# Two heads or two softmaxes at a time in the attentions of a two-block transformer kernel

## The reference

```python
def softmax_attend(q, k, v, scale):
    s = einsum('bqhd,bkhd->bhqk', q, k) * scale
    return einsum('bhqk,bkhd->bqhd', softmax(s), v)

# window heads: |qpos - kpos| <= 128 among latent keys, all 256 context keys, one sink column
p = softmax(concatenate([s_ctx, where(valid, s_band, NEG_INF), sink_col], -1))

def diff_attend(q, k, v, lam, lambda_init, subln_g):
    s = einsum('bqhtd,bkhtd->bthqk', q, k) * HEAD_DIM ** -0.5
    p = softmax(s)
    a = p[:, 0] - lam * p[:, 1]
    o = einsum('bhqk,bkhe->bqhe', a, v)
    return rms_norm(o, subln_g) * (1.0 - lambda_init)
```

## Time and profile before

| | us |
|---|---|
| median of 3 runs | 4892.38 (4888.57 to 4893.21) |
| the profiled execution, device time | 4884.59 |
| its span, first to last instruction | 4882.8 |
| full heads of layer 0, stretch 2941 to 3112 | 171.0 |
| window heads of layer 0, stretch 3112 to 3279.5 | 167.5 |
| differential attention, stretch 4229 to 4363 | 134.0 |

### The profile page before, as it was taken

The page is one execution under the profiler, slowest core; times in us unless marked ns, Lnnn a source line. Parts: engine busy times, 40 slices in busy tenths (PEclk is TensorE's granted clock), DMA queues, the critical chain, the costliest instruction groups (busy, mean ns, idle before and its releaser), DMA issues.

```text
span 4882.8 us, 51549 instructions
## 1 busy us (share of the span) xinstructions
PE 4490.2 (92%) x20694; PEld 3482.8 (71%) x20694; DVE 2612.7 (54%) x4643; ACT 1512.5 (31%) x2535; POOL 1738.0 (36%) x955
## 2 busy tenths in 40 slices
PE   7878989987789999999999899997999979998998
PEld 3667745465668888888888675665888857765886
DVE  4675745368867676754534415654334350484334
ACT  3212211035753232232322324443222232343222
POOL 2244332036954444444444321002222225103442
PEclk9998999998899999999999999988999989998999
DMA  6200200421265554545533200001222112102331
GB/s 219 70 26 14 109 31 31 146 74 62 121 224 173 177 171 162 178 157 174 173 125 129 87 14 21 9 14 39 65 63 68 57 34 61 34 1 62 98 95 48
DMA packets 170762, 441.31 MB, mean 90 GB/s; under 512 B 12219, under 2 KB 78971, under 8 KB 167580
## 3 DMA queue, kind: packets, MB, share of 16 engines
q1 hardware_dynamic: 168060, 422.61, 25.7%
q0 software_dynamic: 2464, 15.41, 0.8%
HBM read 402.32 MB, written 35.65 MB: 90 GB/s over the span
## 4 chain that ended last, share of the span: by engine, by line
PE 68%; DVE 10%; POOL 3%; ACT 2%; issue 1%; DMA 0%; DVEq 0%; ACTq 0%; POOLq 0%
PE psum L254 19%; PE psum L255 19%; PE psum L256 19%; PE psum L260 11%; POOL o L1600 2%; DVE st L2209 2%; PE psum L281 1%; DVE o L1493 1%; DVE Pd L2235 1%; DVE X L1882 0%; ACT P L2280 0%; DVE o L1495 0%; DVE Pe L2233 0%; DVE ffl L1822 0%; DVE rstd L1862 0%
## 5 line engine op out<-in xcount | busy, mean ns | idle before, releaser
L244 POOL TENSOR_TENSOR pair<-raw_ring,pair 128x1024 fp32r<-128x1024 f32 x502 | 1243.2, 2490 | 2063.2 <-ACT pair L236 2063.1
L236 ACT CAST pair<-raw_ring 128x1024 fp32r<-128x1024 f32 x502 | 509.9, 1045 | 374.4 <-PE psum L256 318.6
L254 PE MATMUL psum<-pfh,pair 128*128 128x512 f32 x1152 | 451.7, 392 | 27.3 <-POOL pair L244 26.5
L1675 DVE SCALAR_TENSOR_TENSOR h<-psum,mods,h 128x512 f32<-128x512 f32 x512 | 370.8, 748 | 162.6 <-PE psum L256 160.8
L255 PE MATMUL psum<-pfl,pair 128*128 128x512 f32 x1152 | 449.9, 391 | 0.0
L256 PE MATMUL psum<-pfh,pair 128*128 128x512 f32 x1152 | 449.9, 391 | 0.0
L254 PE MATMUL psum<-ffh,pair 128*128 128x512 f32 (+1 forms) x1056 | 378.3, 358 | 45.7 <-DVE ffl L1822 45.7
L254 PE MATMUL psum<-Ah,pair 128*128 128x512 f32 x1024 | 400.9, 391 | 10.1 <-DVE Al L1670 4.9
L255 PE MATMUL psum<-Al,pair 128*128 128x512 f32 x1024 | 400.4, 391 | 0.0
L256 PE MATMUL psum<-Ah,pair 128*128 128x512 f32 x1024 | 400.2, 391 | 0.0
L255 PE MATMUL psum<-ffl,pair 128*128 128x512 f32 (+1 forms) x1056 | 378.7, 359 | 0.0
(11 more groups left out here) (552 smaller groups left out, 9136.1 us busy)
## 6 DMA issues: line engine op xcount, KB each, us to landing
raw_ring<-wmod SPq DMA_DIRECT2D x144, 512.0 KB, 4.9
raw_ring<-peeru SPq DMA_DIRECT2D x128, 512.0 KB, 4.2
raw_ring<-peerv SPq DMA_DIRECT2D x128, 512.0 KB, 3.9
gates<-stage SPq DMA_DIRECT2D x16, 2048.0 KB, 6.4
Gb<-gates SPq DMA_DIRECT2D x32, 1024.0 KB, 9.2
raw_ring<-win SPq DMA_DIRECT2D x48, 512.0 KB, 4.4
raw_ring<-wgate SPq DMA_DIRECT2D x44, 512.0 KB, 3.5
raw_ring<-wup SPq DMA_DIRECT2D x44, 512.0 KB, 3.6
```

The costliest lines, as they stand in the source:

```text
L236: ac.e.copy(self.pair(t)[0], k.R.of(t)).then_inc(*k.A.up("hi", t))
L244: po.e.tensor_tensor(lo, k.R.of(t), hi.bitcast(F), ALU.subtract).then_inc(*k.G.up("lo", t))
L254: e.matmul(out, w[0], x[0], start=first, stop=False, skip_group_check=True)
L1675: e.scalar_tensor_tensor(out=h[:, j, :], in0=B.of(("down", gi, j)), scalar=m[:, 40 + j, 0:1], in1=h[:, j, :], op0=ALU.mult, op1=ALU.add).t ...
```

## The change

Units of layer 0 become 48 pairs: of the full heads two heads, of the window heads the two key groups kv = 0 and 1 (w = 0 and 1 in the code). Their values go to the two column halves of one output tile, product by product in turn. Where queries and keys are 64 rows deep (window heads and layer 1, `apart`), the score products of w = 0 and w = 1 alternate, so that they use rows 0 to 63 and 64 to 127 in turn. Band masks are added by a product with the identity, and the sink becomes one more score column, also by a product. Scale factors are applied when queries are copied out. The maximum is negated by the reduction itself. ScalarE copies whole transposed rows in layer 0. Output is copied per unit (128 columns) and not per head. Query and key buffers grow to four heads, exponentials to six buffers, transposed rows to three; the first three heads are prepared before the first scores.

In layer 1 nothing is divided by the first softmax's sum: the row becomes e1 + (-lambda x sum1 / sum2) x e2, and the sum enters the epsilon of the norm that follows (three small steps, one each on TensorE, ScalarE and VectorE). For odd units VectorE makes this with one operation, for even units GpSimd makes it with two. Transposes are split in four and two pieces, with the values of unit i-3 between, and all of them share banks 6 and 7, so that the six other banks serve scores alone.

The core of the diff (removed lines are those of the functions printed above and are left out; so are the new buffers):

```diff
+        self.keys = sum(p[3] for p in pieces[0])
+        self.n = self.keys + (sinks is not None)
...
+        return self.st[(2 * i + w) % len(self.st)]
+    def pt(self, i, w):
+        return self.PT[(2 * i + w) % len(self.PT)]
...
+    many = 1 if u.n <= 512 else 2
+    banks = [B.take((key, "s", i, w), many, SIX) for w in range(2)]
+    def masked(w):
+        for c, mk in u.masks:
+            ins = mm(e, banks[w][:, c:c + 128], k.sq["ident"], k.sq[mk], False, True)
+        if u.sinks is not None:
+            ins = mm(e, banks[w][:, u.keys:u.n], k.sq["ident"], u.sinks[w])
+        return ins
+    if u.apart:
+        pe.wait_ge(B.free((key, "s", i, 0)), B.free((key, "s", i, 1)))
+        for j in range(len(u.pieces[0])):
+            for w in range(2):
+                q, kk, c, n = u.pieces[w][j]
+                ins = mm(e, banks[w][:, c:c + n], q, kk)
+                if u.sinks is None and j == len(u.pieces[0]) - 1:
+                    ins.then_inc(*P.up(key, "s", i, w))
+        if u.sinks is not None:
+            for w in range(2):
+                masked(w).then_inc(*P.up(key, "s", i, w))
+    else:
+        for w in range(2):
+            pe.wait_ge(B.free((key, "s", i, w)))
+            for q, kk, c, n in u.pieces[w]:
+                ins = mm(e, banks[w][:, c:c + n], q, kk)
+            ins.then_inc(*P.up(key, "s", i, w))
...
+    dv.e.tensor_reduce(s[:, 0:1], k.B.of((at.key, "s", i, w))[:, 0:at.units[i].n], AX, ALU.max, negate=True).then_inc(*k.V.up(at.key, "m", i, w))
...
+    ac.e.activation(p[:, 0:u.n], k.B.of((at.key, "s", i, w))[:, 0:u.n], AF.Exp, bias=s[:, 0:1], accum_out=total).then_inc(*k.A.up(at.key, "e", i, w))
+    k.B.over((at.key, "s", i, w), k.A.now())
...
+        bank = B.take((key, "pt", i, w), 1 if u.keys <= 512 else 2, SIX)
+        pe.wait_ge(V.at(key, "p", i, w), B.free((key, "pt", i, w)))
+        for c in range(u.keys // 128):
+            ins = turn_in(k, e, bank[:, 128 * c:128 * c + 128], p[:, 128 * c:128 * c + 128])
...
+        ob = B.take((key, "o", i), 1, (6, 7))
+        pe.wait_ge(A.at(key, "pt", i, 0), A.at(key, "pt", i, 1), B.free((key, "o", i)))
+        many = u.keys // 128
+        for c in range(many):
+            for w in range(2):
+                ins = mm(e, ob[64 * w:64 * w + 64, 0:128], u.vals[w][c], at.pt(i, w)[:, 128 * c:128 * c + 128], c == 0, c == many - 1)
+        ins.then_inc(*P.up(key, "o", i))
...
+    for i in range(N + 3):
+        if i < N:
+            prepare(i)
+            tensor_scores(k, pe, at, i, ready(i))
+        if 2 <= i < N + 2:
+            turned(i - 2, 0)
+        if i > 2:
+            values(i - 3)
+        if 2 <= i < N + 2:
+            turned(i - 2, 1)
...
+        dv.wait_ge(A.at(key, "e", i, w))
+        e.reciprocal(s[:, 1:2], s[:, 1:2]).then_inc(*V.up())
+        dv.wait_ge(V.now())
+        e.tensor_scalar(p[:, 0:n], p[:, 0:n], s[:, 1:2], None, ALU.mult).then_inc(*V.up(key, "p", i, w))
...
+        dv.wait_ge(A.at(key, "o", i))
+        e.tensor_tensor(o[1], B.of((key, "o", i))[:, 0:128], o[0].bitcast(F), ALU.subtract).then_inc(*V.up(key, "o", i))
...
+    for i in range(N + 4):
+        if i < N:
+            prepare(i)
+            vector_largest(k, dv, at, i, 0)
+            vector_largest(k, dv, at, i, 1)
+        if 1 <= i < N + 1:
+            weights(i - 1, 0)
+            weights(i - 1, 1)
+        if i > 3:
+            values(i - 4)
...
+        ac.wait_ge(P.at(key, "pt", i, w), P.at(key, "o", before) if before is not None else None)
+        e.copy(at.pt(i, w)[:, 0:n], B.of((key, "pt", i, w))[:, 0:n]).then_inc(*A.up(key, "pt", i, w))
...
+    for i in range(N + 3):
+        first = i >= N or at.units[i].apart
+        if i < N:
+            prepare(i)
+            if not first:
+                exps(i, 0)
+        if 2 <= i < N + 2:
+            turned(i - 2, 0)
+        if i < N:
+            if first:
+                exps(i, 0)
+            exps(i, 1)
+        if 2 <= i < N + 2:
+            turned(i - 2, 1)
+        if i > 2:
+            values(i - 3)
...
+def tensor_differ(k, pe, at):
+    e, P, V, A, G, B, key = pe.e, k.P, k.V, k.A, k.G, k.B, at.key
+    N = len(at.units)
...
+    def turned(i, w):
+        p = at.p(i, 0)
+        if w:
+            pe.wait_ge(A.at(key, "pt", i))
+        else:
+            pe.wait_ge(differed(k, at, i), V.at(key, "pt", i - 1) if i else None)
+        for c in ((0, 1, 2, 3), (4, 5))[w]:
+            ins = turn_in(k, e, tail[:, 128 * (c % 4):128 * (c % 4) + 128], p[:, 128 * c:128 * c + 128])
+        ins.then_inc(*P.up(key, "pt", i, w))
+    def values(i):
+        u = at.units[i]
+        pe.wait_ge(A.at(key, "pt", i), V.at(key, "pt", i), A.at(key, "o", i - 1) if i else None)
+        for c in range(6):
+            ins = mm(e, tail[:, 512:640], u.vals[0][c], at.PT[i % 2][:, 128 * c:128 * c + 128], c == 0, c == 5)
+        ins.then_inc(*P.up(key, "o", i))
+    for i in range(N + 3):
+        if i < N:
+            tensor_scores(k, pe, at, i, None)
+        if 2 <= i < N + 2:
+            turned(i - 2, 0)
+        if i > 2:
+            values(i - 3)
+        if 2 <= i < N + 2:
+            turned(i - 2, 1)
...
+        dv.wait_ge(A.at(key, "e", i, 1))
+        e.reciprocal(s[:, 1:2], s[:, 1:2]).then_inc(*V.up())
+        dv.wait_ge(V.now())
+        e.tensor_scalar(s[:, 1:2], s[:, 1:2], at.sum(i), k.lamb[:, 0:1], ALU.mult, ALU.mult).then_inc(*V.up(key, "c", i))
...
...
+    def difference(i):
+        p, p2 = at.p(i, 0), at.p(i, 1)
+        dv.wait_ge(V.at(key, "c", i), A.at(key, "e", i, 0))
+        e.scalar_tensor_tensor(out=p, in0=p2, scalar=at.s(i, 1)[:, 1:2], in1=p, op0=ALU.mult, op1=ALU.add).then_inc(*V.up(key, "p", i))
+    for i in range(N + 2):
+        if 1 <= i < N + 1:
+            factor(i - 1)
+        if i < N:
+            vector_largest(k, dv, at, i, 0)
+            vector_largest(k, dv, at, i, 1)
+        if 1 <= i < N + 1 and not i % 2:
+            difference(i - 1)
+        if i > 1:
+            turned(i - 2)
+    B.over((key, "tail"), V.now())
...
+    def exps(i, w):
+        if w:
+            scalar_exps(k, ac, at, i, 1, differed(k, at, i - 2) if i > 1 else None, at.s(i, 1)[:, 1:2])
+        else:
+            scalar_exps(k, ac, at, i, 0, P.at(key, "pt", i - 3, 1) if i > 2 else None, at.sum(i))
+    def turned(i):
+        ac.wait_ge(P.at(key, "pt", i, 0), P.at(key, "o", i - 2) if i > 1 else None)
+        e.copy(at.PT[i % 2][:, 0:512], B.of((key, "tail"))[:, 0:512]).then_inc(*A.up(key, "pt", i))
...
     for i in range(N + 3):
         if 2 <= i < N + 2:
             turned(i - 2)
+        if i < N:
+            exps(i, 0)
         if i > 2:
             values(i - 3)
...
+    for i in range(0, len(at.units), 2):
+        p, p2 = at.p(i, 0), at.p(i, 1)
+        po.wait_ge(k.V.at(at.key, "c", i))
+        e.tensor_scalar(p2, p2, at.s(i, 1)[:, 1:2], None, ALU.mult).then_inc(*G.up())
+        po.wait_ge(G.now(), k.A.at(at.key, "e", i, 0))
+        e.tensor_tensor(p, p, p2, ALU.add).then_inc(*G.up(at.key, "p", i))
```

357 lines of the change are left out of this document (151 added, 206 removed).

## The result

The changed kernel took 4765.1 us (median of 4 runs, 4763.3 to 4770.2) where the kernel before took 4890.7 (4 runs, 4888.6 to 4893.2): a ratio of 0.9745, interval 0.9728 to 0.9762. The forecast was 4841, its range 4790 to 4880.

A forecast was written before the change was run, and what follows sets the result against it. TensorE was taken to bound the full heads and differential attention, no engine's throughput the window heads. Full heads -12, window heads -25, differential attention -14 gave -51 from 4884.6: 4833.6, plus 7.8 to the median: 4841, range 4790 to 4880.

The forecast's parts named there:

- What bounds the kernel: Three attentions: TensorE bounds full heads and differential attention; window heads are bound by no engine's throughput, with clock 0.82.
- Changing row halves: Alternating score products: each change saves the earlier instruction's length less 0.16 us: 0.27 after 512 columns, 0.05 after 256.
- The next one begins only after its load, 0.16 later: Scores on TensorE: the other row half starts 0.16 us after the last instruction, where serial would be 0.215.
- One change is in the trace: Differential attention's scores: one row-half change, at 4285.52 to 4286.11, was read as showing how the halves overlap.
- the -14 forecast for the differential attention: Layer 1: a unit falls from 4.86 to 4.42 us by alternating scores, less 0.10 for split transposes, times 32.
- Changing column halves: Values of layer 0: alternating column halves gains nothing; bounds were half the values' time gained or a shape-change cost per product.
- that bound of -37: Full heads: best case against the forecast -12, with values at half time, 112 products-of-two saving 0.22 each, -25.
- Window heads: Layer 0: a pair of groups takes 34.8 us against 41, -25 in all, with the clock near 1.00.
- GpSimd as the bound: Differential attention rival: GpSimd's two operations exceed 5.5 us instead of 3.5; at 7 us, 4865 in all; no separate chance.
- about 5.5 between factor and transpose: Differential attention: time available to hide GpSimd's two operations of 3.5 us in every second unit.
- Halves overlap in full: Rival, all attentions: row and column halves stream together; differential -24, full heads -37, window heads -45, 4786; chance 23%.
- The rival by which column alternation costs 0.2 us each: Layer 0 values: 400 products pay 0.20 us each for alternating column halves, +80, 4921; chance 7%.

The follow-up runs named there:

- run 4: Kernel before, with layer 1's scores taking both score banks first and alternating between row halves: 4896.1 us, 1.0027 of before.
- run 6: Kernel before, with ScalarE copying all 768 columns of transposed weights in the differential attention, VectorE none: 4876.8 us, 0.9979 of before.
- run 2: Changed kernel with the alternating scores put in serial order, one row half after the other: 4779.7 us, 0.9789 of before.
- run 5: Changed kernel with GpSimd's share undone, VectorE forming all 32 differences: 4759.4 us, 0.9731 of before.
- run 11: Changed kernel, all differences on VectorE, seven of eight output squares on GpSimd, ScalarE's exponential before its copy in window heads: 4751.9 us, 0.9719 of before.
- Run 1: Changed kernel with layer 0's values in serial order, all of head 0, then all of head 1: 4792.8 us, 0.9814 of before.
- run 17: Kernel before, with four useless identity transposes added on TensorE in each of 48 window-head units: 4871.9 us, 0.9971 of before.
- run 12: Changed kernel with the window heads' sinks handled by small VectorE and ScalarE steps instead of products: 4753.3 us, 0.9723 of before.
- run 16: Edits of run 11 and run 12 on the changed kernel, but ScalarE's window-head order left as in the changed kernel: 4748.4 us, 0.9713 of before.
- run 15: Changed kernel with full-head values in blocks of two or three products per column half instead of strict alternation: 4767.2 us, single run.
- run 13: Changed kernel with the edits of run 11 and run 12 together: 4753.4 us, 0.9714 of before.

## Why the prediction was right or wrong

**What bounds the kernel: wrong for the differential attention, right for the other two.** The step "The differential attention is TensorE's again: 4.86 of 4.86 us in one unit, VectorE 4.48 close behind" failed. I read the busy shares there and the chain of waits only in the window heads. Runs 4 and 6 showed it: half the time on the scores made the stage 10 us longer, and VectorE's copy taken away made it 9 shorter.

**Changing row halves: wrong.** "The next one begins only after its load, 0.16 later" took the end of a wait for a property of the array, and its 0.16 was worked out wrongly: the start was at 4285.58, 0.06 after the instruction before. "One change is in the trace" was wrong as well: the first unit of the same stage, from 4211.76 on, has all eight instructions in pairs. Where the bank is free, the starts are 0.01 us apart. But the terms that hung on it were also wrong in their place: of the -14 forecast for the differential attention, the order gives 0.0 (run 2). The 21.9 us that were measured are what came off VectorE's sequence (the scaling, 0.63, three small steps of 0.14 to 0.17 and their hand-overs, about 1.1 us a unit: 33.5 us in run 5), less the 11.6 by which the kernel with GpSimd's share is behind. The overlap itself, which serial order keeps, was taken away by no run. It is needed: in run 11 TensorE's own sequence fills the 3.72 us of a unit, and with 2.7 us for the scores instead of 1.5 it would be an estimated 4.9.

**Changing column halves: wrong, the largest single miss.** "I take no gain" stands against both heads in the time of one. 112 product pairs at 0.22 are the 24.6 us that the bound had, and the full heads met that bound of -37 to a microsecond: -37.7. Run 1 shows 13.8 of the 24.6 as the worth of the order; the other 10.8 follow from TensorE taking instructions four places ahead, which serial order keeps. What remains, 37.7 - 24.6 = 13.1, is the idle time (from 5.7 to 2.2 us, where I forecast 5 less) and, with 9.6 where I forecast 7, the grouping, which no run isolates.

**Window heads: mechanism right, sizes off.** TensorE busy for most of the time (99.3 of 113.3 us), the clock at 1.00, and stalls for both exponentials (8 of up to 1.2 us) came as said. A pair of groups took 113.3 / 4 = 28.3 us instead of 34.8. Scores and values at half time would take 4.3 and 4.85 us off a pair, 9 in all; 6.5 were seen, as TensorE now stands idle for 14 of the 113.3 us. The clock's return, which the forecast had at 39 - 32 = 7 us a pair, 28 in all, is some 22 of the 52.9 us by the estimate under run 17. The masks were costed on TensorE alone and their place in the loop at nothing: they are worth 15 us there, a good part of it with the clock. The sinks were costed as work of 2.6 us and not weighed against the small steps they replace: runs 12 and 16 show -9 us without them. The grouping of two heads was not isolated by any run.

**GpSimd as the bound: the rival had the wrong condition.** "Its pair would have to take over 5.5 us instead of 3.5." It took 4.0 (2.21 and 1.81, where I had 1.62 and 1.9) and already cost 10 to 11.6 us. The step "about 5.5 between factor and transpose" was too long: the timeline of one such unit has GpSimd's first operation start at 4177.88, right after the factor, and TensorE done with the scores that stand ahead of the transposes at 4181.28. That is 3.4 us, and the transposes start at 4182.02, when GpSimd is done.

**The rivals.** "Halves overlap in full", 4786, came nearest: -24, -37 and -45 against -21.9, -37.7 and -52.9. Its full-head term was right for the reason given. Its window term has the overlap right, and nothing for the masks' place in the loop. Its differential term has the overlap right, but took TensorE for the bound of the kernel before: that it agrees within 2 us is luck, as two effects that it did not have, VectorE's relief and GpSimd's latency, made the 21.9. The remaining 21 us to 4765 are 8 in the window heads, less 2 in the differential attention, 8.2 of pace in the feed-forward stage, which no reading of the trace of before could give, and the 7.8 that I added for the distance from the profiled execution to the median, which the profiled execution of the changed kernel doesn't have. Of the Trainium skill, the page TensorEngine Tiling was cited for parallel tiles (Tiling Modes, Key Properties); the trace now agrees with 0.01 us between the starts of both kinds of halves.

The rival by which column alternation costs 0.2 us each is excluded: its change costs nothing that the trace shows.

## What to carry to other kernels

Before pricing an edit on the engine that looks full, follow the chain of waits in that very stage: an engine that is fed by another at a steady pace shows as busy all the time, and a product of the second half that begins late may be waiting for its bank. Work moved off a chain of small dependent steps can be worth its whole latency even when it goes to the busiest engine, as with the masks; price both sides, for with the sinks it was the other way round. Work given to an idle but slow engine costs its latency. Keep products of two halves of the array within four instructions of each other, and look for a place where both already run together before assuming that they can't. Waiting for both banks at once pays only where that wait closes no longer loop (run 4 lost 10 us to it). And when a stage gets shorter on TensorE, look at the granted clock again, as pauses can take the gain back.

## What the runs showed of the hardware that I had not expected

- Products on two halves of the array, by rows or by columns, stream at the same time, in fp32 with two instructions each: starts 0.01 us apart, 24 instructions of 128 columns in 1.26 us, where twelve for one head take 1.25.
- TensorE starts an instruction for the other half up to four places ahead of its turn, before earlier ones of the first half (runs 1 and 15; run 2 agrees).
- Instructions of 256 columns in a stage of 640 us follow each other by 113.3 or by 117.9 ns from one execution to the next of the same kernel, about 7 us in all.
- GpSimd needs 2.21 us for a multiplication by a column's value over 768 columns, and 1.62 for a multiplication and an addition in one operation of the same size elsewhere in the kernel before. VectorE is busy beside both; the cause was not tested.
- A little useless work in TensorE's pauses, 21 us of it, made a kernel 16 us faster by the medians (run 17), and two edits that each saved time let the clock fall when put together (run 13).
- One stage of the same code took 166.2, 167.7 and 172.0 us at granted clocks of 0.82, 0.81 and 0.78 (before, runs 4 and 6).
